# A hybrid backbone layer on eight cores: block 0 of the first feed-forward without its down products, and the latents' second norm woven into the context's projections

## The chip, the cores and the metric

One Trainium2 chip, all 8 NeuronCores, one program. Each core does its own share and none talks to another. The metric is the device time of one execution in microseconds (us), which is that of the slowest core. A core has TensorE (PE, matmuls), VectorE (DVE), ScalarE (ACT), GpSimd (POOL) and SyncE (SP). POOL and SP also issue the DMAs. Each engine runs its own list of instructions strictly in order.

## What is computed

One layer of a diffusion backbone on 8192 context tokens and 8192 latent tokens of width 1024:

```
x += 0.5 * gate1 * SwiGLU1(mod(rmsnorm(x)))                  # FF1, hidden width 2816
h  = mod(rmsnorm(x)); [p | q | k | v | gate logits] = h @ w_in
A  = PoolMixer(p) @ w_br_pool                                # centred mean over 2/4/8/16 tokens
B  = Attn(q, k, v) @ w_br_att                                # context: dense; latent: neighbourhood + cache
x += gate2 * ((sig_A * A + sig_B * B) @ w_out)
x += 0.5 * gate3 * SwiGLU2(mod(rmsnorm(x)))                  # FF2
```

`mod` is a scale and a shift per channel that come from a conditioning vector (`ada` weights). The outputs are x of both kinds of tokens and the context's k and v.

## The kernel before

**Tiles.** A core holds 1024 context tokens (half 0), 1024 latent tokens (half 1) and 256 neighbouring latent tokens. They stand as five token tiles: 0 and 1 are context, 2 and 3 latents, 4 the 256 neighbours (`TT_ALL`). x lies transposed, channels on partitions, in eight chunks of 128 channels per tile: `XT[0..3]` in f32, `XH` for tile 4. `XN` holds the normed input of the next products in bf16. All of it, with the scratch, is one SBUF tensor, `arena`; PSUM is `ps`, eight banks of 512 f32 columns. Sharing of memory is kept by `P.claim`, which hands the waits of the old users to the new ones.

**Order of the work.** Python code emits the instructions of all engines; `P.emit` adds the semaphore waits that reads and writes need. An engine's order is the order of emission. Where two strands shall overlap, they are generators: `weave` (line 210) draws from a side strand in proportion to the cost of the main one, and `pump` (line 729) draws so many steps.

**Weights.** `plan` writes one list of 512 KB weight units; a ring of eight slots is filled in that order by POOL's DMA queue. `wacq` takes the next unit, `wrel` frees its slot, and the load into the slot waits for the last matmul that read it. Units 0 to 7 are ada weights; 8 and 9 are the gate and up weights of FF1's block 0, 10 to 13 ada weights, 14 its down weights, 15 to 17 those of block 1.

**A norm** (`norm_gen`, line 620) of a tile squares the eight chunks into `XN` (ACT, DVE or POOL by the string `sq`), sums them on PE with eight matmuls against ones (`norm_stat`, in bank 4 or 5), takes Ln and Exp on ACT, multiplies each chunk with the result on DVE or POOL into one of two buffers (`scaled`), and applies scale and shift from there into `XN` on ACT or DVE (`modulated`). ACT must load a table when it goes from Silu to Ln and when it goes back.

**Feed-forward** (`ff_phase`, line 723). The hidden width is cut in 11 blocks of 256. For a block and a tile, `ff_GU` makes the gate and up products of one 128-wide part `jj` (16 matmuls of 512 columns in two banks of 0 to 3), ACT takes Silu, DVE multiplies into `HB` (two slots). `ff_DN` makes the down products: for each of eight output chunks `m` two matmuls into a bank of `poolDN` (4 to 7), which DVE adds into x (`vstt`, line 430). Within a block, step s emits GU(s, 0), DN(s-1) chunks 0 to 3, GU(s, 1), DN(s-1) chunks 4 to 7. In FF1's block 0 x is still being loaded by SP's queue (`load_x_tile`, each tile after a given weight unit has landed), and the norm of tile s+1 is emitted inside step s. In FF1's last block, a tile that is done (`tile_done`) is spilled to DRAM and its second norm joins the side strands.

**Mixer** (`mixer`, line 1226). It first runs out the norms of tiles up to 2 (`left[0][0] <= 2`), then weaves: the context's q projection with the norms of tiles 3 and 4; the context's k and v projections with its pool branch (`p_gen(0)`); the latents' q, k, v projections (pool `d2`, banks 4, 5, 6) with the context's attention (`ctx_att`, banks 0 to 3); then the merge of the context and the latents' attention, and so on. A q or k product (`qk_gen`, line 834) is a group of eight matmuls in a bank; ACT squares it; `finish` of the group before it is emitted right after: one matmul with `ONESBLK` (pool `s2`, bank 7), Ln and Exp on ACT, and a `vstt` on DVE that reads the group's bank last. q, k and v of the two halves lie in the memory of x tiles that have been spilled: half 0 in that of tiles 2 and 3, half 1 in that of tiles 0 and 1.

In the traces, line 413 is `mm`, line 410 `mm` of attention, 422 `actv`, 426 `vtt`, 430 `vstt`, 603 `ptt` (POOL), 323 a weight load, 555 a load of x.

## Time and profile before

| | us |
|---|---|
| median of 3 runs (lowest, highest) | 1688.76 (1687.05, 1701.29) |
| the profiled execution's own time | 1701.97 |
| span of its slowest core, core 3 | 1700.4 |
| span of its core 0 | 1685.8 |

The page of the profile is of core 3. In this execution cores 2 and 3 had a lower granted clock than the other six, whose spans are 1680.7 to 1686.5 us; stretches below are read on core 0. Times in the rows are us from the span's start. A row of a timeline names the engine, the line and shape, the count of instructions merged, and in brackets how long the engine had been idle and what ended that.

### The profile page before, as it was taken

What the parts mean: (1) busy time and instruction counts of PE and PEld (TensorE: products, weight loads), DVE (VectorE), ACT (ScalarE), POOL (GpSimd) and SP (SyncE); (2) the same over time, 40 slices, a digit from 0 to 9 for tenths busy, and PEclk for the clock granted to TensorE, in tenths of its full rate; (3) what the DMA queues carried; (4) which work ended last, traced back from release to release, by engine and by line L of the source; (5) the groups of instructions that cost most, each with busy time, mean ns of one, the idle gap of its engine ahead of it and who ended that gap; (6) DMA issues with size and microseconds to landing.
All of it is one profiled execution on the core that took longest, in us unless ns stands there. A gap on an engine that the chain in (4) does not pass through costs nothing.

```text
span 1700.4 us, 25281 instructions; the slowest of 8 cores (1680.7 to 1700.4 us)
## 1 busy us (share of the span) xinstructions
PE 1536.0 (90%) x8548; PEld 695.4 (41%) x8548; DVE 956.5 (56%) x1646; ACT 494.2 (29%) x739; POOL 158.2 (9%) x235
## 2 busy tenths in 40 slices
PE   1689999999999995698889888999999999999998
PEld 1234444444444442243434444444334444444443
DVE  2256556555566554464546665345366666666666
ACT  2651110111111125745636566235421111111110
POOL 2131000000000012300000000021210000000000
PEclk9799999999999997787889899999999999999999
DMA  9906442345432332457225355584322222222005
GB/s 183 243 1 91 75 67 37 48 74 76 75 48 43 59 87 99 101 116 142 37 56 120 99 113 113 138 186 75 50 38 38 37 38 38 38 38 38 13 1 198
DMA packets 35788, 134.68 MB, mean 79 GB/s; under 512 B 5072, under 2 KB 5200, under 8 KB 33616
## 3 DMA queue, kind: packets, MB, share of 16 engines
q0 software_dynamic: 22560, 79.88, 30.3%
q1 hardware_dynamic: 13104, 53.18, 9.3%
q8 instruction: 73, 1.20, 0.3%
q14 instruction: 51, 0.42, 0.1%
HBM read 191.95 MB, written 20.97 MB: 125 GB/s over the span
## 4 chain that ended last, share of the span: by engine, by line
PE 79%; DVE 6%; issue 5%; ACT 4%; DMA 4%; POOL 1%; DVEq 0%; ACTq 0%; SPq 0%; POOLq 0%
PE ps L413 76%; ACT arena L422 3%; DVE arena L430 3%; PE ps L410 3%; DMA arena<-wts 3%; DVE arena L426 2%; POOL arena L603 1%; DMA arena<-xin 1%; DVE arena L436 1%; ACT L422 1%; DVEq L183 0%; DVE arena L445 0%; DVE arena L442 0%; ACTq L183 0%; POOL arena L323 0%
## 5 line engine op out<-in xcount | busy, mean ns | idle before, releaser
L413 PE MATMUL ps<-arena 128*128 128x512 bf16 (+3 forms) x7108 | 1476.7, 363 | 132.9 <-DVE arena L430 53.5
L413 PEld LDWEIGHTS ps<-arena 128*128 128x128 bf16 x7108 | 646.7, 100 | 919.6 <-issue 336.8
L430 DVE SCALAR_TENSOR_TENSOR arena<-ps,arena 128x512 f32<-128x512 f32 (+2 forms) x860 | 562.5, 714 | 89.6 <-ACT arena L422 47.1
L422 ACT ACTIVATE arena<-ps 128x512 f32<-128x512 f32 (+4 forms) x418 | 266.1, 652 | 1045.8 <-PE ps L413 526.7
L426 DVE TENSOR_TENSOR arena<-arena,ps 128x512 bf16<-128x512 f32 (+1 forms) x198 | 130.2, 658 | 411.7 <-PE ps L413 382.4
L426 DVE TENSOR_TENSOR arena<-arena 128x512 f32<-128x512 f32 (+10 forms) x196 | 141.6, 738 | 114.9 <-ACT arena L422 89.3
L323 POOL DMA_DIRECT2D arena<-wts x150 | 79.9, 536 | 1255.5 <-PE ps L413 1025.0
L422 ACT ACTIVATE arena<-arena 128x512 bf16<-128x512 f32 (+6 forms) x230 | 165.6, 748 | 86.9 <-DVE arena L426 25.0
L410 PE MATMUL ps<-arena 128*128 128x65 bf16 (+3 forms) x1440 | 80.6, 214 | 25.5 <-DVE arena L436 16.0
L603 POOL TENSOR_TENSOR arena<-arena 128x512 bf16<-128x512 f32 (+3 forms) x77 | 75.9, 1010 | 186.4 <-ACT arena L422 99.3
L410 PEld LDWEIGHTS ps<-arena 64*128 64x128 bf16 (+1 forms) x1440 | 53.5, 98 | 79.0 <-issue 69.8
L430 DVE SCALAR_TENSOR_TENSOR arena<-arena,ps 128x512 f32<-128x512 f32 x64 | 43.8, 684 | 51.0 <-PE ps L413 45.3
L436 DVE TENSOR_SCALAR arena<-ps,arena 128x64 bf16<-128x64 f32 (+1 forms) x136 | 38.0, 280 | 18.7 <-PE ps L413 3.6
L422 ACT ACTIVATE arena<-ps,arena 128x512 f32<-128x512 f32 (+2 forms) x66 | 43.5, 664 | 13.5 <-PE ps L413 12.5
L422 ACT ACT_TABLE_LOAD x25 | 32.1, 1283 | 46.2 <-PE ps L413 43.2
L442 DVE CAST arena<-ps 128x128 bf16<-128x128 f32 (+2 forms) x58 | 22.3, 391 | 19.7 <-PE ps L410 11.3
L442 DVE COPY arena<-ps 128x512 f32<-128x512 f32 x16 | 11.0, 687 | 7.1 <-PE ps L413 3.7
L442 DVE CAST arena<-arena 128x512 bf16<-128x512 f32 x16 | 6.8, 425 | 9.1 <-ACT arena L422 8.1
L430 DVE SCALAR_TENSOR_TENSOR arena<-arena 128x1024 bf16<-128x1024 f32 (+1 forms) x14 | 10.8, 770 | 1.0 <-DVE arena L426 0.2
L426 DVE TENSOR_TENSOR arena<-ps,arena 128x6 f32<-128x6 f32 (+2 forms) x20 | 3.3, 165 | 14.1 <-PE ps L413 13.1
L445 DVE RECIPROCAL arena<-ps 128x2 f32<-128x2 f32 (+1 forms) x48 | 8.0, 167 | 0.8 <-PE ps L410 0.8
L438 DVE TENSOR_SCALAR arena<-arena 128x512 bf16<-128x512 f32 x4 | 1.9, 542 | 0.1
(12 smaller groups left out, 6.1 us busy)
## 6 DMA issues: line engine op xcount, KB each, us to landing
arena<-wts POOLq DMA_DIRECT2D x150, 512.0 KB, 8.8
arena<-xin SPq DMA_DIRECT2D x8, 1024.0 KB, 13.6
xspill<-arena SPq DMA_DIRECT2D x4, 2048.0 KB, 7.0
arena<-xspill SPq DMA_DIRECT2D x4, 2048.0 KB, 14.7
yoT<-arena SPq DMA_DIRECT2D x32, 256.0 KB, 2.3
arena<-ebias SPq DMA_DIRECT2D x12, 640.0 KB, 5.1
arena<-ebias SPq DMA_DIRECT2D x8, 768.0 KB, 5.4
nkT<-arena SPq DMA_DIRECT2D x8, 256.0 KB, 2.9
```

What stands on the lines that cost most here:

```text
L323: wtok.append(P.emit("pool", lambda e: e.dma_start(out=WR[:, s, :], in_=src), writes=[wslot_res[s]], dma_sem="w%d" % s))
L410: return P.emit("pe", lambda e: e.matmul(out, lhsT=lhsT, rhs=rhs, start=start, stop=stop, skip_group_check=True), reads=reads, writes=writ ...
L413: return P.emit("pe", lambda e: e.matmul(out, lhsT=lhsT, rhs=rhs, start=start, stop=stop), reads=reads, writes=writes, inc=inc)
L422: return P.emit("act", lambda e: e.activation(out=out, in_=in_, func=func, **kw), reads=reads, writes=writes)
L426: return P.emit("dve", lambda e: e.tensor_tensor(out=out, in0=in0, in1=in1, op=op), reads=reads, writes=writes)
L430: return P.emit("dve", lambda e: e.scalar_tensor_tensor(out=out, in0=in0, scalar=scalar, in1=in1, op0=op0, op1=op1), reads=reads, writes=w ...
L436: return P.emit("dve", lambda e: e.tensor_scalar(out=out, in0=in0, scalar1=s1, scalar2=None, op0=op0), reads=reads, writes=writes)
L438: return P.emit("dve", lambda e: e.tensor_scalar(out=out, in0=in0, scalar1=s1, scalar2=s2, op0=op0, op1=op1), reads=reads, writes=writes)
L442: return P.emit("dve", lambda e: e.tensor_copy(out=out, in_=in_), reads=reads, writes=writes)
L445: return P.emit("dve", lambda e: e.reciprocal(out=out, in_=in_), reads=reads, writes=writes)
L603: return P.emit("pool", lambda e: e.tensor_tensor(out=out, in0=in0, in1=in1, op=op), reads=reads, writes=writes)
```

## The change

It has two parts, made together.

*FF1 block 0.* All five tiles' gate and up products are made without down products between them; their hidden values go to `HB5` (slots 2 to 6), and the down products (`owed`) are emitted in block 1, chunk by chunk beside block 1's own. In block 0 the squares of a tile are emitted two tiles ahead, those of tile 1 ahead of tile 0's Ln; `modulated` alternates between ACT and DVE. The loads of x tiles wait for earlier units, that of tile 1 for a later one. The four ada units of the hook are used after all of block 0's products.

*Second norm.* In FF1's last block only tiles 0 and 1 (context) are normed. The norms of tiles 2, 3 and 4 are woven into the context's q, k and v projections. The memory is swapped to allow it: half 0's q, k, v lie over x tiles 0 and 1, half 1's over 2 and 3. The context's pool branch moves into the weave with the latents' projections and the context's attention; there the latents' projections keep banks 4 and 5, and the pool branch has bank 6. The context's projections have banks 0 to 3 where they had 0 to 5. A norm with a gap takes bank 4 alone, and down products use banks 5 to 7 while a norm may be beside them and in each last block.

```diff
-        for nm in ("q", "k", "p", "v"):
+        for nm in ("q", "k", "v"):
             plan_win(0, nm)
-        for nm in ("q", "k", "v"):
-            plan_win(1, nm)
+        plan_win(1, "q")
+        plan_win(0, "p")
+        plan_win(1, "k")
+        plan_win(1, "v")
...
+        HB5 = mem(oG + 16384, 10240, BF16, "p (t j n) -> p t j n", t=5, j=2)
...
-            b = stat if stat is not None else norm_stat(tile)
+            b = stat if stat is not None else norm_stat(tile, 4 if gap else None)
...
+        def hbuf(hs):
+            return (HB, "hb", hs) if hs < 2 else (HB5, "hb5", hs - 2)
...
         poolDN = PsumPool(P, [4, 5, 6, 7], "DN")
+        poolDN3 = PsumPool(P, [5, 6, 7], "DN3")
...
-                while k > 0 and side:
+                while k > 0 and side and not (lazy_load is not None and side[0][0] > 1):
...
-                for ti, u in ((1, 6), (2, 10), (3, 13), (4, 15)):
+                for ti, u in ((1, 7), (2, 9), (3, 10), (4, 11)):
                     lazy_load(ti, after=wtok[u])
+                norm_tile(nidx, tiles[1], part="a", sq="apv")
                 norm_tile(nidx, tiles[0], part="b", mo="av", stat=stat0, mid=lambda: first_mod(acc))
...
+                if first:
+                    for t in range(ntt):
+                        ff_GU(G, U, rg, ru, nj, tiles[t], 2 + t, jjs=[0])
+                        if t + 2 < ntt:
+                            norm_tile(nidx, tiles[t + 2], part="a", sq="pppapppa")
+                        if t + 1 < ntt:
+                            norm_tile(nidx, tiles[t + 1], part="b", mo="av")
+                        ff_GU(G, U, rg, ru, nj, tiles[t], 2 + t, jjs=[1])
+                    wrel(ug)
+                    wrel(uu)
+                    blk0_hook()
+                    owed = wacq(("ffd", which, bi))
+                    after_block(bi)
+                    continue
...
-                        if first and step + 1 < ntt:
-                            norm_tile(nidx, tiles[step + 1], sq="a" if step == 0 else "pppppppa",
-                                      sc="vvvp" if step else "v")
-                        if first and step == 1:
-                            blk0_hook()
-                            ud, Dn, rd = wacq(("ffd", which, bi))
...
+                        if owed is not None and step < ntt:
+                            ff_DN(owed[1], owed[2], nj, tiles[step], 2 + step, ig, ms=[m])
                         if step >= 1:
                             ff_DN(Dn, rd, nj, tiles[step - 1], (step - 1) % 2, ig, ms=[m],
-                                  chunk_done=chunk_done if last else None)
-                            pump(3 if last else 2)
+                                  chunk_done=chunk_done if last else None, spare=bool(side) or last)
+                            pump(2)
...
-            while left and left[0][0] <= 2:
+            while left and left[0][0] < 2:
                 run_all(left.pop(0)[1])
...
-            d1, s1 = PsumPool(P, [0, 1, 2, 3, 4, 5], "d1"), PsumPool(P, [6, 7], "s1")
-            weave(qk_gen(0, "q", d1, s1), 16.0, side, 40.0)
...
-            weave(chain_gens(qk_gen(0, "k", d1, s1), v_gen(0, d1)), 30.0, p_gen(0, d1), 21.0)
...
+            d1, s1 = PsumPool(P, [0, 1, 2, 3], "d1"), PsumPool(P, [6, 7], "s1")
+            weave(chain_gens(qk_gen(0, "q", d1, s1), qk_gen(0, "k", d1, s1), v_gen(0, d1)), 46.0, side, 78.0)
...
-            d2, s2 = PsumPool(P, [4, 5, 6], "d2"), PsumPool(P, [7], "s2")
-            weave(chain_gens(qk_gen(1, "q", d2, s2), qk_gen(1, "k", d2, s2), v_gen(1, d2)), 54.0, ctx_att(), 32.0)
+            d2, s2 = PsumPool(P, [4, 5], "d2"), PsumPool(P, [7], "s2")
+            weave(weave_gen(chain_gens(qk_gen(1, "q", d2, s2), qk_gen(1, "k", d2, s2), v_gen(1, d2)), 54.0,
+                            p_gen(0, PsumPool(P, [6], "d2p")), 21.0), 75.0, ctx_att(), 32.0)
...
-            return norm_gen(1, TT_ALL[ti], sc="vvvp", gap=4)
+            if ti < 2:
+                return norm_gen(1, TT_ALL[ti], sq="pppa", sc="vvvp", gap=4)
+            return norm_gen(1, TT_ALL[ti], sq="p", sc="vvvp", mo="av", gap=4)
```

ACT at the start, before: the small one is the conditioning vector's Silu, the four that follow are tile 0's squares, then Ln (`ps,arena`), Exp and four `modulated` of tile 0, Silu, and the eight squares of tile 1.

```order
L422 ACTIVATE arena<-arena 128x16
L422 ACTIVATE arena<-arena 128x512 x4
L422 ACTIVATE arena<-ps,arena 128x512
L422 ACTIVATE arena<-arena 128x512 x5
L422 ACTIVATE arena<-ps 128x512
L422 ACTIVATE arena<-arena 128x512 x8
```

The same place after the change (lines have moved by two):

```order
L424 ACTIVATE arena<-arena 128x16
L424 ACTIVATE arena<-arena 128x512 x7
L424 ACTIVATE arena<-ps,arena 128x512
L424 ACTIVATE arena<-arena 128x512 x5
L424 ACTIVATE arena<-ps 128x512
L424 ACTIVATE arena<-arena 128x512 x2
```

Three squares of tile 1 now stand ahead of tile 0's Ln, where none did.

PE at the first weave of the latents' projections with the context's attention, before: `128x256 x4` are score products, `128x65 x8` products with v, `128x128 x2` transposes, `128x512 x9` a group of eight for q with the `ONESBLK` matmul of the group before it.

```order
L410 MATMUL ps<-arena 128x256 x4
L413 MATMUL ps<-arena 128x512 x9
L410 MATMUL ps<-arena 128x256 x4
L413 MATMUL ps<-arena 128x512 x9
L410 MATMUL ps<-arena 128x65 x8
L413 MATMUL ps<-arena 128x512 x9
L410 MATMUL ps<-arena 128x256 x4
L413 MATMUL ps<-arena 128x512 x9
L410 MATMUL ps<-arena 128x65 x8
L410 MATMUL ps<-arena 128x128 x2
```

The same place after the change; `x8` is a group of the pool branch, `x17` and `x18` are two groups of q in a row.

```order
L412 MATMUL ps<-arena 128x256 x4
L415 MATMUL ps<-arena 128x512 x17
L412 MATMUL ps<-arena 128x256 x4
L415 MATMUL ps<-arena 128x512 x9
L412 MATMUL ps<-arena 128x65 x8
L415 MATMUL ps<-arena 128x512 x8
L412 MATMUL ps<-arena 128x256 x4
L415 MATMUL ps<-arena 128x512 x18
L412 MATMUL ps<-arena 128x65 x8
L412 MATMUL ps<-arena 128x128 x2
```

Some neighbouring q groups have a pool group between them, others only attention products, and some nothing.

## Rows read from the trace of the kernel before

**Rows 1.** The page: busy time and share, and PE and its clock in 40 slices.
```profile
PE 1536.0 (90%) x8548; PEld 695.4 (41%) x8548; DVE 956.5 (56%) x1646; ACT 494.2 (29%) x739; POOL 158.2 (9%) x235
...
PE   1689999999999995698889888999999999999998
...
PEclk9799999999999997787889899999999999999999
```

**Rows 2.** Busy time by stretch, core 0 (length, then each engine, clock, DMA).
```profile
604.00:694.00 90.00, 64.70 (x273) 27.87 (x277) 45.98 (x79) 44.91 (x65) 24.22 (x23) 0.85 0.29 101
694.00:776.00 82.00, 67.28 (x282) 28.87 (x286) 47.72 (x76) 49.48 (x85) 11.80 (x19) 0.92 0.50 107
776.00:832.00 56.00, 46.50 (x311) 21.35 (x314) 26.26 (x72) 41.47 (x68) 3.12 (x7) 0.94 0.53 97
```

**Rows 3.** Timeline of core 0, the first tiles of FF1's block 0.
```profile
32.67 4.90 DVE L426 TENSOR_TENSOR arena<-arena 128x512 f32<-128x512 f32 x8 [8.69 <-ACT arena L422]
...
35.66 19.62 SPq L555 DMA_DIRECT2D arena<-xin  x4
...
38.62 0.57 PE L413 MATMUL ps<-arena 128*128 128x2 bf16 x16 [2.33 <-DMA arena<-wts]
...
44.00 3.19 PE L413 MATMUL ps<-arena 128*128 128x512 bf16 x7 [4.82 <-ACT arena L422]
...
49.41 2.75 PE L413 MATMUL ps<-arena 128*128 128x512 bf16 x12 [2.22 <-DMA arena<-wts]
...
53.56 2.19 ACT L422 ACTIVATE arena<-arena 128x512 bf16<-128x512 f32 x4 [2.32 <-DMA arena<-xin]
```

**Rows 4.** The same timeline: tile 2's wait for x, down products' `vstt`, end of block 0.
```profile
72.84 0.63 ACT L422 ACTIVATE arena<-arena 128x512 bf16<-128x512 f32 x1 [3.45 <-DMA arena<-xin]
...
86.83 14.04 PE L413 MATMUL ps<-arena 128*128 128x512 bf16 x51 [4.82 <-DVE arena L426]
...
88.15 2.73 DVE L430 SCALAR_TENSOR_TENSOR arena<-ps,arena 128x512 f32<-128x512 f32 x4
...
133.62 0.59 POOL L323 DMA_DIRECT2D arena<-wts  x1 [8.26 <-PE ps L413]
...
141.47 0.60 ACT L422 ACTIVATE arena<-ps 128x512 f32<-128x512 f32 x1 [7.80 <-PE ps L413]
```

**Rows 5.** The same timeline, tile 1's norm: table load, Ln, Exp, first and last chunks.
```profile
56.55 1.28 ACT L422 ACT_TABLE_LOAD   x1 [0.81 <-PE ps L413]
...
57.85 0.69 ACT L422 ACTIVATE arena<-ps,arena 128x512 f32<-128x512 f32 x1
...
58.63 0.63 ACT L422 ACTIVATE arena<-arena 128x512 f32<-128x512 f32 x1
59.36 1.29 DVE L426 TENSOR_TENSOR arena<-arena 128x512 f32<-128x512 f32 x2 [7.26 <-ACT arena L422]
...
65.47 1.52 ACT L422 ACTIVATE arena<-arena 128x512 bf16<-128x512 f32 x2 [0.25 <-DVE arena L426]
```

**Rows 6.** Timeline of core 0, FF1's last block around GU(3, 0).
```profile
644.54 0.60 ACT L422 ACTIVATE arena<-ps 128x512 f32<-128x512 f32 x1
...
645.31 0.69 DVE L426 TENSOR_TENSOR arena<-arena,ps 128x512 bf16<-128x512 f32 x1 [3.63 <-ACT arena L422]
...
646.81 7.89 PE L413 MATMUL ps<-arena 128*128 128x512 bf16 x23 [3.97 <-DVE arena L430]
```

**Rows 7.** Timeline of core 0: a dense stretch of PE, then latents' projections beside the context's attention.
```profile
720.78 21.11 PE L413 MATMUL ps<-arena 128*128 128x512 bf16 x95 [0.69 <-ACT arena L422]
...
783.75 0.60 ACT L422 ACTIVATE arena<-ps 128x512 bf16<-128x512 f32 x1 [0.30 <-PE ps L413]
...
785.89 0.74 DVE L430 SCALAR_TENSOR_TENSOR arena<-ps,arena 128x512 bf16<-128x512 f32 x1
...
791.33 0.52 PE L410 MATMUL ps<-arena 128*128 128x65 bf16 x10 [2.12 <-DVE arena L442]
...
791.68 3.77 PE L413 MATMUL ps<-arena 128*128 128x512 bf16 x9
```

80 lines of the change are left out of this document (44 added, 36 removed).

## The prediction

> **What bounds the kernel now.** I read the page first. PE is busy 90% of the span, and in its 40 slices it dips in two places: the first three slices, and slices 15 to 17 (600 to 720 us), where the granted clock dips too [rows 1]. So outside these PE sets the pace, and work moved there costs its own length. The table by stretches says how much is to be had: from 604 to 694 us, FF1's last block with the second norms, PE is busy 64.7 of 90 us, and 67.3 of 82 in the context's projections after it; in the next stretch, the latents' projections with the context's attention, 46.5 of 56 [rows 2]. The count of matmuls gives the rest. A dense matmul of 512 columns takes 0.222 us (95 in 21.11) [rows 7]. From 603.6 to 776.5 PE has 532 of them or their like (216 of the block, 36 sums for norms, 280 for q, k, v, p), 118 us of 172.9. So 55 us are waiting or half clock.
>
> The timelines name the waits. In FF1's last block, GU(3, 0)'s Silu stands on ACT behind all eight `modulated` of a norm and a table load; DVE waits 3.63 us for that Silu and behind it hold all evictions, so PE waits 3.97 us for a bank, and its next 23 matmuls take 7.89 us, 0.34 each [rows 6]. At the start, tile 0's first product begins at 44.0 and the up weights come at 49.4 (2.22 us of waiting), x of tile 1 is whole at 53.6, x of tile 2 at 72.8 [rows 3, 4]. Block 0 ends at 140.0: the first Silu of block 1 is at 141.5, after eight gate products (1.7 us) [rows 4].
>
> **The start.** Tile 1's load now waits for unit 7 instead of 6. Unit 7 landed at 38.6, where the last ada matmuls run; the first of the four loads of tiles 1 and 2 was issued at 35.66, when unit 6 was there [rows 3]. That is 2.9 us; unit 7 lands a little sooner without x beside it, so I take x of tile 1 whole 2 us later, at 55.6. That would harm nothing, but ACT now has three squares of tile 1 ahead of tile 0's Ln, and DVE two of them ahead of tile 0's `scaled`, and the last ones need the second half of x. Before, Ln and the eight `scaled` were done under the ada loads (32.7 to 37.6) [rows 3]. Now they come in a row: square 0.6, table, Ln and Exp 2.8 [rows 5], eight `scaled` 4.9, biases and four `modulated` on ACT 4.1 (they lie in PE's wait of 4.82 before 44.00) [rows 3], to 68.0. Eight up matmuls at 0.43 (the rate after 44.00, too [rows 3]) end at 71.4; it was about 51.
>
> Then the norm of the next tile bounds each step: eight sums, table with Ln and Exp 2.8, eight chunks 7.6 (59.4 to 67.0) [rows 5], eight up matmuls. Half the chunks on DVE don't shorten this: DVE then has two `scaled` and a `modulated` per pair, about what ACT had. Sums and up products take 1.8 us each dense and 3.4 at half clock; I take 2.5 and 3. The first step ends at 87.5 (x of tile 2, 73 us, comes in time), two more of 15.7 at 119, the 256 columns of tile 4 need 10, the last products and the ada matmuls 5: block 0 ends at 134, 6 us earlier than now. At full clock it is 126, at half throughout 139.
>
> What is owed: 4.5 tiles by 16 matmuls are 72 by 0.222 = 15.8 us, in block 1, where PE is dense. DVE must take two evictions where it took one, 16 by 0.68 [rows 4] and two products of 0.69 = 12.3 us per tile against PE's 64 by 0.222 = 14.2: covered for the big tiles, short by some 1.3 us for tile 4. Block 1's up weights wait for the slot of block 0's gate weights. Before, that load was issued at 133.6 and was there when needed 7.8 us later [rows 4], under down products; now only up products, ada matmuls and a gate group cover it, some 5 us: 2 us lost (0 to 4). Sum for the start: -6 + 15.8 + 1.3 + 2 = **+13.1 us** (+5 to +19).
>
> **The second norm.** In the last block norms 0 and 1 stay, at fewer steps per chunk, so Silu(3, 0) stands behind three `modulated` and not eight. By hand from these durations: PE waits 4.7 us and loses 1.7 to the clock in step 3, some 8.5 in step 4 and at the evictions of the end. 232 matmuls are 51 us, with that 66: the block ends at 669.6 instead of about 693. Then q, k, v of the context with norms 2, 3, 4. ACT has Square, Ln, Exp per group, 1.9 us, and a norm's Ln, Exp and four `modulated` of 0.76 [rows 5], 4.4 us in 7.4 groups (its 25 steps at 78/46 steps per unit of cost, a group being 2): 2.5 us per group, where PE has 2.2. So 16 groups take 40 us at ACT's pace, the eight of v 16 at PE's: 56, to 726. The next stretch starts 50 us earlier. But the pool branch, 72 matmuls or 15.8 us, is not yet done: **-34.2 us** (-40 to -26). Four banks instead of six don't bind here.
>
> **The latents' projections with two banks.** This is the price. A q or k group's bank is read last by `vstt`, which is emitted after the next group. From the next group's end to the end of that `vstt` the trace has Square at 783.75 to `vstt`'s end at 786.63, 2.9 us [rows 7]. With three banks another group of 1.75 us and attention products lay between; with banks 4 and 5 the group after next waits for it. What is woven between is 0.2 (`ONESBLK`) and 0.4 to 0.7 of attention, and a pool group of 1.75 us in about five places of 14 (the second order of PE shows both kinds). So a period is 2.9 + 1.75 = 4.65 us, where 20 groups had 56 us, 2.8 each, and some 2 us of PE stand idle in most. No row of before shows such a row of waits. From below: at the full clock, 14 by 4.65, the first two groups 3.9, four groups of 256 columns by 3.2: 82 us against the 56 now [rows 2], less seven pool groups absorbed (12.2), +13.6. From above: after a gap of 2.12 us the next nine matmuls took 3.77 us, half clock [rows 7]; if each unfilled wait does that, 9 periods of 6.4, 5 of 5.9, with the rest 108 us, and 0.6 us per period for `vstt` behind the pool branch's long DVE adds: +48. I take five half-clock groups (8.5 us), 0.3 us of DVE queue per period (4), and 2 us for pool mixes that share one bank: 82 + 8.5 + 4 + 2 - 56 - 12.2 = **+28 us**.
>
> The Trainium skill, "TensorE: Matmul & The Clock Gate", on the failure mode called psum-queue depth-cycling, says that cycling through PSUM banks with small idles between groups makes the clock oscillate and costs throughput. The row of 2.12 us agrees; by that rule the second rival below would be the case. "Perfetto Trace Analysis", on matmuls, says that groups should rotate through banks so that eviction overlaps the next group. Two banks do rotate; by that rule there would be no loss (the first rival), but the rows make eviction longer than the next group.
>
> **Sum.** Core 0's span 1685.8 and 1.6 around it (1701.97 - 1700.4) are 1687.4, 1.4 under the median 1688.76. 13.1 - 34.2 + 28 = +6.9, so 1695.7. FF2's last block with three banks is bound by the same DVE evictions as with four: 0 to 2 us, taken as 0.
>
> **Rivals.**
> *The two banks cost nothing to speak of.* Pool and attention work fills the waits, as the DVE and ACT are only half busy there. For it: PE is idle 9.5 us of the 56 now anyway [rows 2]. Against: five fills for 14 periods. The third term is then +2: 13.1 - 34.2 + 2 = -19.1, 1669.7. An earlier x of tile 1 would go the same way.
> *Half clock after each two-bank wait.* The place is the latents' q and k. It decides from the point where an unfilled wait keeps the clock down as the 2.12 us did: a wait of 0.69 us ahead of the dense stretch did not [rows 7], and I expect some 2.2. The third term is +48: +26.9, 1715.7.
> *ACT holds the context's projections.* If q, k, v with three norms takes 70 us and not 56, for `modulated` ahead of Square and PE waiting for POOL's squares, the second term is -20: +21.1, 1709.9. For it: ACT and PE are within 15% there.
> That the change does not do what it says: the orders show it does, but the squares ahead of tile 0's Ln undo block 0's gain; that is in the forecast.
>
> **How the numbers follow.** Forecast 0.50 (its own range 1680 to 1706), no bank cost 0.17, half clock 0.23, ACT 0.10. What a measurement of this kernel can tell from no change is about 1%, 17 us: 1672 to 1706. The forecast lies within it, the first rival under, the two others over: faster 0.17, same 0.50, slower 0.33. The range runs from just under the first rival to just over the second: 1668 to 1718.
>
> **What would show it.** Right: tile 0's Ln after 55 us and its gate products near 65; block 1's first Silu between 128 and 140, and block 1 some 15 us longer than block 2; the first score products of attention near 740 (726 and the start's 13); then PE idle 2 us before most q and k groups with `vstt` (L432) as releaser, and more L415 matmuls of 0.43 us. Wrong: Ln of tile 0 at 32; a stretch of latents' projections under 75 us; or score products of attention after 755.

## The result, and the profile after

| | before | after |
|---|---|---|
| runs compared, us | 1687.05, 1688.76, 1701.29 | 1749.22, 1750.65 |
| median of all four, us | 1695.03 | 1780.08 |
| ratio of the runs compared, 95% interval | | 1.034 (1.0227 to 1.0453) |
| span of core 0, us | 1685.8 | 1733.3 |
| span of the slowest core, us | 1700.4 | 1747.7 |

The change makes the kernel slower by 3.4%. The prediction was 1695.7, range 1668 to 1718: wrong, and outside the range. (The medians of all four hold runs, 1823.58 before and 1809.51 and 1942.15 after, in which the cores of one die had a lower clock; the ratio leaves them out, and the table by run leaves out the rest of e4's profiled execution for the same reason.)

The page after, of core 6, answers to [rows 1]: PE is busy 87% where it was 90%, its second slice stands at 2 instead of 6, and seven slices from 655 us on stand at 6 or 7, where two stood at 5 and 6.

```profile
PE 1525.1 (87%) x8391; PEld 695.1 (40%) x8548; DVE 983.0 (56%) x1682; ACT 465.5 (27%) x693; POOL 173.4 (10%) x245
...
PE   1278999999999997777677889899999999999998
...
PEclk9978999999999998888889999899999999999999
```

The same table by stretch as [rows 2], core 0 after, cut at these marks: first Silu of FF1's block 1, of block 2, of the last block; the context's first Square; the first score product of the context's attention; the first of the latents' attention; the end.

```profile
0.00:142.30 142.30, 62.38 (x394) 29.01 (x400) 51.34 (x90) 47.45 (x66) 36.42 (x48) 0.76 0.60 131
142.30:217.20 74.90, 70.02 (x364) 30.55 (x371) 55.08 (x92) 5.55 (x11) 4.71 (x9) 0.98 0.35 60
217.20:631.10 413.90, 397.79 (x2219) 194.21 (x2256) 248.16 (x422) 44.37 (x81) 23.77 (x45) 0.98 0.37 62
631.10:700.10 69.00, 56.08 (x252) 24.58 (x256) 39.84 (x63) 27.50 (x38) 19.55 (x20) 0.90 0.38 127
700.10:771.10 71.00, 56.24 (x227) 23.38 (x230) 35.21 (x57) 43.07 (x71) 29.12 (x33) 0.88 0.43 106
771.10:910.40 139.30, 94.14 (x547) 42.44 (x558) 71.70 (x166) 56.32 (x88) 7.09 (x13) 0.89 0.30 60
910.40:1733.30 822.90, 775.10 (x4396) 347.37 (x4480) 480.07 (x794) 240.99 (x341) 52.73 (x79) 0.98 0.33 74
```

These marks cut every run below in the same way; this is the table to keep at hand (core 0, us; "after" predicted is what the prediction's terms make of before: its stages come 0.8 over its sum of +6.9, as it cut the stages a little elsewhere). "2 to 9" are the eight blocks between block 1 and the last. What each run changes is told in the sections below.

| run | block 0 | block 1 | 2 to 9 | last | context | latents | rest | ratio to before (95%) |
|---|---|---|---|---|---|---|---|---|
| before | 141.5 | 50.7 | 413.2 | 93.3 | 77.9 | 86.3 | 823.0 | |
| after, predicted | 135.5 | 69.8 | 413.2 | 66 | 56 | 130.1 | 823.0 | 1.004 |
| after | 142.3 | 74.9 | 413.9 | 69.0 | 71.0 | 139.3 | 822.9 | 1.034 |
| e1 block 0's part alone | 145.5 | 76.8 | 414.3 | 93.1 | 79.6 | 86.7 | 821.9 | 1.0197 (1.0181 to 1.0212) |
| e5 | 139.2 | 77.9 | 414.4 | 93.3 | 77.9 | 86.2 | 821.8 | 1.0146 (1.0098 to 1.0195) |
| e16 | 128.9 | 75.1 | 417.4 | 93.0 | 79.5 | 86.7 | 821.2 | 1.0064 (1.0029 to 1.0099) |
| e6 | 147.7 | 81.3 | 414.3 | 93.3 | 77.9 | 86.6 | 819.6 | 1.0195 (1.0127 to 1.0263) |
| e15 | 145.0 | 68.6 | 412.3 | 93.1 | 79.6 | 86.7 | 820.8 | 1.0113 (1.0076 to 1.015) |
| e2 second norm's part alone | 139.6 | 51.4 | 412.3 | 68.5 | 72.8 | 141.2 | 824.4 | 1.0166 (1.0128 to 1.0204) |
| e8 | 139.6 | 50.7 | 410.0 | 68.5 | 72.8 | 132.3 | 824.6 | 1.0105 (1.0069 to 1.0141) |
| e10 | 138.8 | 51.8 | 415.1 | 69.0 | 74.3 | 137.2 | 824.4 | 1.0119 (1.0051 to 1.0186) |
| e12 | 139.9 | 52.5 | 412.6 | 68.5 | 72.8 | 120.8 | 823.2 | 1.0043 (1.0031 to 1.0056) |
| e11 | 139.8 | 52.5 | 412.7 | 68.5 | 118.5 | 69.7 | 825.0 | 1.0011 (0.9979 to 1.0042) |
| e13 | 140.2 | 50.7 | 409.9 | 68.5 | 115.4 | 64.5 | 822.4 | 0.9943 (0.9927 to 0.9959) |
| e20 | 140.6 | 51.8 | 412.1 | 68.5 | 114.7 | 65.0 | 823.9 | 0.9877 (0.9857 to 0.9897) |
| e17 before, early read | 139.8 | 51.5 | 412.2 | 93.3 | 80.7 | 81.3 | 825.4 | 0.992 (0.9902 to 0.9938) |
| e14 | 143.0 | 52.5 | 415.3 | 69.7 | 114.0 | 64.9 | 823.5 | 0.9943 (0.9925 to 0.9961) |
| e22 | 140.6 | 52.5 | 412.5 | 68.5 | 124.6 | 65.1 | 823.8 | 1.0016 (1.0007 to 1.0025) |
| e21 | 133.9 | 72.7 | 415.2 | 69.9 | 114.3 | 65.0 | 822.5 | 1.003 (1.0018 to 1.0042) |
| e3 | 146.3 | 75.2 | 412.6 | 69.9 | 108.3 | 83.6 | 824.0 | 1.0236 (1.0219 to 1.0253) |
| e4 two banks alone | 140.4 | 50.7 | 410.0 | 93.3 | 77.9 | 131.9 | | 1.0276 (1.0256 to 1.0297) |

Each ratio is taken against runs of the kernel before made beside it. Their median was 1687.96 beside e1 to e4, 1690.72 beside e5, e6, e8 and e10, 1691.14 beside e11 to e14, 1702.45 beside e15, e16, e17 and e20, and 1689.95 beside e21 and e22; the ratios of e15, e16, e17 and e20 therefore flatter by some 0.7%.

The table also shows how far a stage moves where nothing was changed in it: the context's stage of before's order is 77.9 or 79.6 us, block 0 of before's order lies between 138.8 and 143.0, and blocks 2 to 9 between 409.9 and 417.4. Smaller differences than these say nothing.

The prediction was made from core 0. Its 47.5 us are 25.7 up to the last block, -24.3 in that block, -6.9 in the context's stage and +53.0 in the latents' stage. In that execution core 0 is the fastest core of all: block 0 ends at 142.3 there and at 144.6 to 146.8 on the others, whose spans reach 1747.7. This is why the timed difference (61 us against the median of the three, 1688.76) is larger than core 0's.

### The profile page after: what moved, and what is told of

The parts are those of the page before. It is cut to its first block, busy times and chain, and to the rows that moved or that the text cites. A ratio compares the mean times of both kernels' runs of the same rounds, so it can differ in the third digit from the quotient of the medians.

```text
span 1747.7 us, 25134 instructions; the slowest of 8 cores (1733.3 to 1747.7 us)
## 1 busy us (share of the span) xinstructions
PE 1525.1 (87%) x8391; PEld 695.1 (40%) x8548; DVE 983.0 (56%) x1682; ACT 465.5 (27%) x693; POOL 173.4 (10%) x245
## 4 chain that ended last, share of the span: by engine, by line
PE 75%; DVE 8%; issue 7%; ACT 5%; DMA 3%; POOL 2%; DVEq 0%; another core or an unknown queue 0%; ACTq 0%; SPq 0%; POOLq 0%
PE ps L415 72%; ACT arena L424 4%; DVE arena L432 4%; PE ps L412 3%; DVE arena L428 3%; DMA arena<-wts 2%; POOL arena L607 1%; DMA arena<-xin 1%; DVE arena L438 1%; ACT L424 1%; DVE arena L440 0%; POOL arena L323 0%; DVEq L183 0%; DVE arena L444 0%
## 5 line engine op out<-in xcount | busy, mean ns | idle before, releaser
L415 PE MATMUL ps<-arena 128*128 128x512 bf16 (+2 forms) x6951 | 1461.4, 362 | 197.2 <-ACT arena L424 76.7
L428 DVE TENSOR_TENSOR arena<-arena 128x512 f32<-128x512 f32 (+10 forms) x204 | 150.4, 757 | 122.2 <-ACT arena L424 65.5
L424 ACT ACTIVATE arena<-arena 128x512 bf16<-128x512 f32 (+6 forms) x184 | 137.9, 765 | 117.5 <-DMA arena<-xin 48.0
L607 POOL TENSOR_TENSOR arena<-arena 128x512 bf16<-128x512 f32 (+3 forms) x87 | 90.9, 1070 | 160.3 <-ACT arena L424 66.0
L412 PE MATMUL ps<-arena 128*128 128x65 bf16 (+3 forms) x1440 | 80.4, 214 | 20.7 <-DVE arena L438 15.8
L424 ACT ACTIVATE arena<-ps,arena 128x512 f32<-128x512 f32 (+2 forms) x66 | 43.4, 663 | 14.8 <-PE ps L412 5.4
L424 ACT ACT_TABLE_LOAD x25 | 32.1, 1283 | 45.9 <-PE ps L415 42.8
L440 DVE TENSOR_SCALAR arena<-arena 128x512 bf16<-128x512 f32 (+1 forms) x32 | 19.9, 629 | 6.0 <-POOL arena L607 3.4
L428 DVE TENSOR_TENSOR arena<-ps,arena 128x6 f32<-128x6 f32 (+2 forms) x20 | 3.3, 165 | 13.6 <-PE ps L415 12.6
L447 DVE RECIPROCAL arena<-ps 128x2 f32<-128x2 f32 (+1 forms) x48 | 8.0, 166 | 1.1 <-PE ps L412 1.0
## 6 DMA issues: line engine op xcount, KB each, us to landing
arena<-xspill SPq DMA_DIRECT2D x4, 2048.0 KB, 11.8
```

Source lines behind the costliest of these rows:

```text
L412: return P.emit("pe", lambda e: e.matmul(out, lhsT=lhsT, rhs=rhs, start=start, stop=stop, skip_group_check=True), reads=reads, writes=writ ...
L415: return P.emit("pe", lambda e: e.matmul(out, lhsT=lhsT, rhs=rhs, start=start, stop=stop), reads=reads, writes=writes, inc=inc)
L424: return P.emit("act", lambda e: e.activation(out=out, in_=in_, func=func, **kw), reads=reads, writes=writes)
L428: return P.emit("dve", lambda e: e.tensor_tensor(out=out, in0=in0, in1=in1, op=op), reads=reads, writes=writes)
L440: return P.emit("dve", lambda e: e.tensor_scalar(out=out, in0=in0, scalar1=s1, scalar2=s2, op0=op0, op1=op1), reads=reads, writes=writes)
L447: return P.emit("dve", lambda e: e.reciprocal(out=out, in_=in_), reads=reads, writes=writes)
```

## The experiments

### Each half alone, and the two banks alone

e1 is block 0's part with the rest as before, e2 the rest with block 0 as before. e3 gives the latents' projections three banks again and weaves the pool branch with the context's v. e4 is the kernel before with one list changed:

```diff
-            d2, s2 = PsumPool(P, [4, 5, 6], "d2"), PsumPool(P, [7], "s2")
+            d2, s2 = PsumPool(P, [4, 5], "d2"), PsumPool(P, [7], "s2")
```

> Block 0 in two parts with its down products in block 1, alone; last block, context's projections and latents' projections as before. Core 0 of the kernel before ends at 1685.8 us; in the changed kernel the first Silu of the last block comes 25.7 us later (631.1 against 605.4). Theory (the three terms stand apart, and this one is 25.7 us): core 0 ends near 1711, some 1.5% over the kernel before. Rival (a part of the 25.7 us is lost only because the last block follows it differently, or is made up later by weights that are there sooner): under 1700, or over 1720.

> Second norm between the context's projections, pool branch and two banks in the latents' projections, with block 0 as before. Theory (terms stand apart): the last block ends some 24 us sooner, context's q, k, v take 71 us without the pool branch, the latents' stage 139 us: -24.3 - 6.8 + 53.0 = +22, core 0 ends near 1708, and together with the block 0 run the two differences make the 47.5 us of both at once. Rival (they interact, for instance by the clock or by when weights come): the sum of both differences is off by over 8 us.

> The changed kernel, but the latents' projections have banks 4, 5, 6 again and the pool branch is woven with the context's v instead of the latents' projections (norms 2, 3, 4 lie between the context's q and k only). Theory (two banks made the 37 us net of the latents' stage): that stage goes from 139 us back to some 86, the context's stage grows by the pool branch's 15.8 us and little else (71 to 87-92): core 0 ends at 1733.3 - 53.0 + 16 to 21 = 1696 to 1701. Rival (the stage is long for the pool branch's adds on DVE or for the clock, not for banks): the stage with three banks stays over 105 us or the adds cost as much beside v; end over 1712.

> The kernel before with banks 4 and 5 instead of 4, 5, 6 for the latents' projections, nothing else changed (bank 6 idle). The stage from the first score product of the context's attention to the first of the latents' is 86.3 us in the kernel before, 56 of it projections. Theory (each bank is read last by vstt 2.9 us after the next group's end, period 4.65 us): without the pool branch's groups between them at least 14 periods lose about 1.8 us: +26 us if at the full clock, up to +50 if the half clock follows; I expect +35, core 0 ends near 1721. Rival (the two banks are covered by attention and it is the pool branch, its one bank and its DVE adds that make the stage long): +10 or less, end under 1697.

Measured: in the timed runs the halves add up. They lie 33 and 25 us over those of the kernel before, together 58 of the 61. On core 0 alone they don't: 32.1 and 24.5 against the 47.5 of both, 9 us off. e1's own term on core 0 is 31 us, not 25.7, like the other cores of the change; core 0 did better than these in the one profiled execution after.

e4 is the clearest of the four: one bank fewer, and the stage goes from 86.3 to 131.9 us, +45.6 where +35 was expected, with nothing else in it. The timed runs say the same (1734.7 and 1735.3 against 1688). For the same matmuls PE's busy time goes from 71.8 to 89.0 us and its idle time from 14.5 to 42.9, so 17 of the 45.6 us are the clock. e3's latents' stage is back at 83.6, as that theory has it, but its context's stage is 108.3 instead of the 87 to 92 expected; core 0 ends at 1719.9, 13 us sooner than with the change (the timed runs lie 22 us lower), where 32 to 37 were expected. The pool branch costs more than its 15.8 us of products beside v, too: at its end PE waits 6.55 us for its adds on DVE. So a part of e3's rival held: the adds cost as much beside v.

### What the latents' stage waits for

PE after, core 0, the first periods of the latents' q (the timeline's columns as in [rows 7]):

```profile
782.93 2.10 PE L415 MATMUL ps<-arena 128*128 128x512 bf16 x9 [0.48 <-DVE arena L447]
787.81 2.10 PE L415 MATMUL ps<-arena 128*128 128x512 bf16 x9 [2.78 <-DVE arena L432]
...
792.69 2.99 PE L415 MATMUL ps<-arena 128*128 128x512 bf16 x9 [2.41 <-DVE arena L447]
...
803.61 3.65 PE L415 MATMUL ps<-arena 128*128 128x512 bf16 x9 [2.45 <-DVE arena L432]
```

From group to group 4.88 us (782.93 to 787.81, 787.81 to 792.69), with a wait of 2.4 to 2.8 us for the `vstt` that reads the bank two groups back, and then nine products in 3.0 to 3.65 us in some and 2.1 in others. (L447, named in two rows, is the attention's reciprocal right behind that `vstt` on DVE. The `vstt` ends at 792.54 and PE starts 0.15 us later, as it does at 787.81 behind the one that ends at 787.66.) Is it the number of banks, or how late that read is issued? e8 makes 4, 5 and 6 one pool for both kinds of groups. e12 leaves the banks as they are and issues the read earlier:

```diff
                             mm(bank_ap(b)[:, 0:n], W[:, kc, bb * 128:(bb + 1) * 128], XN[:, kc, t0:t0 + n],
                                kc == 0, kc == 7, [rw, rxn(kc, t0)], [banks[b]], inc=(kc == 7))
+                            if kc == 3 and half == 1 and pend:
+                                finish(pend.pop(0))
```

> The run with the second norm's part alone, with one edit: banks 4, 5 and 6 are one pool that the latents' projections and the pool branch share, instead of 4, 5 for the one and 6 for the other; the order of all engines is the same. That run's stage from the context's first score product to the latents' first takes 141.2 us (86.3 before, without the pool branch's 15.8); with two banks alone and no pool branch it took 131.9. Theory (the third use of a bank, 2.9 us behind the next group, is what makes it wait; a third bank removes most waits): stage 104 to 112 us, timed 1677 to 1684, faster than the kernel before. Rival (the pool branch's adds on DVE and the mix through ACT hold the evictions, whatever the banks): 125 us or more, timed over 1696.

> The run with the second norm's part alone (two banks for the latents' projections, one for the pool branch), with one edit: in the latents' q and k the sum over a head's squares, Ln, Exp and vstt of a group are issued behind the fourth product of the next group instead of behind its eighth. Nothing else moves. The stage took 141.2 us there. With three banks shared it still took 132.3, so the number of banks is not the whole of it. Theory (what counts is how late the read that frees the bank is issued and done, 2.9 us behind the next group's end): four products are 0.9 us, in some 14 periods, and fewer stretches at the lower clock: stage 122 to 131 us. Rival (the evictions are late for other work on ACT or DVE, not for the order on PE): stage within 3 us of 141.

e8 fell short: 132.3 us, where 104 to 112 were expected. With a pool group between two q groups, three shared banks are two again; this is read from the order, not tested by itself. (By the order of emission, two of the latents' k groups in e8 and e10 read their successor's sums: where two pool mixes lie between them, they have the same bank. The times are read with that in mind; the order of work is the same.)

e12 is the answer: 120.8 us instead of 141.2, for four matmuls of order. (On ACT the move does a little more: Ln and Exp of a group now stand ahead of the next group's Square.) From group to group it is 3.80 us (760.20 to 764.00 below) where it was 4.88 after the change. The table by stretches for this stage, core 0, first e2:

```profile
744.70:885.90 141.20, 98.23 (x548) 43.61 (x558) 71.00 (x164) 55.57 (x87) 7.10 (x13) 0.85 0.31 59
```

and e12 (this window begins 0.7 us ahead of its mark; at the mark the busy time is 86.3 and the clock the same):

```profile
745.50:866.30 120.80, 86.42 (x548) 40.13 (x557) 72.05 (x167) 55.97 (x88) 7.10 (x13) 0.96 0.37 72
```

The same 548 matmuls are in both. PE's idle time falls from 43.0 to 34.4 us, 8.6, less than 14 times 0.9; the matmuls themselves fall from 98.2 to 86.4 us, 11.8, as the granted clock of the stretch rises from 0.85 to 0.96. The greater part of this gain was the clock, which the shorter waits gave back. e12's rows show waits of 1.3 to 1.6 us with full speed behind them:

```profile
752.11 2.10 PE L415 MATMUL ps<-arena 128*128 128x512 bf16 x9 [1.39 <-DVE arena L432]
...
760.20 2.10 PE L415 MATMUL ps<-arena 128*128 128x512 bf16 x9 [1.64 <-DVE arena L432]
...
764.00 2.10 PE L415 MATMUL ps<-arena 128*128 128x512 bf16 x9 [1.34 <-DVE arena L447]
```

The Trainium skill, "TensorE: Matmul & The Clock Gate", has this under psum-queue depth-cycling: small idles between groups that cycle through banks make the clock oscillate. The trace agrees in part: the clock was 0.85 with waits mostly of 2.3 to 2.8 us and 0.96 with mostly shorter ones, but not every such wait was followed by half clock (787.81 above).

The stage has a second part, which neither run touches. Its q and k products end at 832.6 before and at 868.5 after; behind that only v, the attention and, after, the rest of the pool branch are left. Before:

```profile
776.50:832.60 56.10, 46.27 (x310) 21.42 (x316) 26.19 (x71) 41.98 (x69) 3.02 (x6) 0.94 0.53 97
832.60:862.80 30.20, 25.51 (x167) 11.44 (x171) 19.08 (x56) 6.09 (x8) 1.06 (x2) 0.90 0.31 53
```

and after, with PE's two long waits of the second part:

```profile
771.10:868.50 97.40, 64.70 (x368) 29.43 (x374) 46.72 (x108) 47.61 (x77) 4.45 (x8) 0.89 0.28 59
868.50:910.40 41.90, 29.44 (x179) 13.01 (x184) 24.97 (x60) 8.71 (x12) 2.64 (x5) 0.88 0.34 64
```

```profile
883.73 2.10 PE L415 MATMUL ps<-arena 128*128 128x512 bf16 x9 [1.93 <-ACT arena L424]
...
895.57 4.00 PE L415 MATMUL ps<-arena 128*128 128x512 bf16 x9 [5.14 <-ACT arena L424]
```

So of the stage's 53.0 us, 41.3 lie in the q and k part and 11.7 in the other. The two waits are for the pool branch's last mixes: ACT reads their one bank after DVE has done the branch's adds (888.53 to 893.80), the same chain as the 6.55 us in e3. In the whole stage PE's idle time grew by 30.6 us and its busy time by 22.4, of which 15.5 are the pool branch's 72 products at full clock: on this core the clock cost some 7 us more than before.

### The context's stage

e10 (on e8) takes the `modulated` of norms 2 to 4 off ACT, e14 (on e13, below) gives half their squares to DVE, e20 (on e13) gives the context's projections five banks and the early read.

```diff
-            return norm_gen(1, TT_ALL[ti], sq="p", sc="vvvp", mo="av", gap=4)
+            return norm_gen(1, TT_ALL[ti], sq="p", sc="vvvp", mo="v", gap=4)
```

> The run with shared banks, with one more edit: the modulated chunks of norms 2, 3 and 4 (between the context's projections) all on DVE instead of half on ACT. The context's stage took 72.8 us without the pool branch in the run with the second norm's part alone, PE waiting for ACT before 2.6, 2.1, 2.7 and 2.1 us at its single products (the sum of squares per head, which needs Square). Theory (Square stands behind modulated on ACT): the stage shortens by 4 to 8 us against the shared banks' run. Rival (PE waits for the norm's own chain, POOL's squares and Ln, or the work only changes the engine): within 2 us, or longer, since DVE's scaled and modulated then stand ahead of vstt.

> Those two edits, and the squares of norms 2, 3 and 4 half on DVE and half on POOL instead of all on POOL (1.0 us each). In the context's stage (72.8 us) PE waits 0.6 to 0.8 us ahead of single products of the norm's sum, for POOL's squares. Theory (POOL's squares pace the sums): stage shorter by 3 to 6 us. Rival (ACT is what paces the stage, with Square, Ln, Exp and modulated in one queue): within 2 us.

> The run with the pool branch beside the latents' q and the early read there, with two more edits: the early read in the context's q and k too, and five banks (0, 1, 2, 3, 5) instead of four for the context's projections. The stage with q, k, v and three norms took 72.8 us of the 115.4 us from the context's first Square to the latents' first score product. Theory (the late read with four banks paces the context's stage, not ACT's modulated or POOL's squares): 5 to 10 us less, timed 1673 to 1678. Rival (the chain of each norm, from squares to modulated, paces it): within 2 us of that run.

None of the three moved it by much: 74.3 instead of 72.8 in e10; 114.0 and 114.7 instead of 115.4 with q and pool branch in e14 and e20. (Read to the latents' first Square, which leaves most of q and the pool branch out, e14's stage is 72.0 where runs with the same order there have 74.3 to 76.1, so some 3 us shorter; but PE's waits in it add up to 14.8 us against 14.7 in e13, and what shrank is its busy time.) What PE waits for merely changes its name. In e2 (the timeline of ACT and PE, first fence) it waits for ACT's Square, which stands behind a `modulated` that itself waited for DVE; in e10 (PE, second fence) for DVE's `vstt`, which stands behind `modulated` and `scaled` there.

```profile
688.63 0.81 ACT L424 ACTIVATE arena<-arena 128x512 bf16<-128x512 f32 x1 [1.50 <-DVE arena L428]
...
690.07 0.38 PE L415 MATMUL ps<-arena 128*128 128x512 bf16 x1 [2.63 <-ACT arena L424]
```

and e10:

```profile
695.37 2.10 PE L415 MATMUL ps<-arena 128*128 128x512 bf16 x9 [1.57 <-DVE arena L432]
...
729.43 1.89 PE L415 MATMUL ps<-arena 128*128 128x512 bf16 x8 [3.63 <-DVE arena L432]
```

After, PE waits 11.6 us for ACT and 2.8 for POOL in this stage and is busy 56.2 of 71.0 us at a clock of 0.88, while ACT is busy only 43.1. That the chain of a norm through POOL, PE, ACT and DVE, in queues shared with Square and `vstt`, sets the 71 us is what remains; it was not tested by itself and stays open.

### Block 0: squares ahead of a norm

After, ACT and DVE at tile 0's norm, core 0:

```profile
49.29 1.15 ACT L424 ACTIVATE arena<-arena 128x512 bf16<-128x512 f32 x2 [25.59 <-DMA arena<-xin]
55.08 0.63 ACT L424 ACTIVATE arena<-arena 128x512 bf16<-128x512 f32 x1 [4.65 <-DMA arena<-xin]
55.73 1.28 ACT L424 ACT_TABLE_LOAD   x1
57.02 0.69 ACT L424 ACTIVATE arena<-ps,arena 128x512 f32<-128x512 f32 x1
```

then DVE's `scaled`:

```profile
58.53 6.59 DVE L428 TENSOR_TENSOR arena<-arena 128x512 f32<-128x512 f32 x8 [2.75 <-ACT arena L424]
```

ACT waits 25.59 us for x of tile 1 with tile 0's Ln behind it in the queue. e5 moves tile 1's squares behind tile 0's norm, and e16 in addition the squares of tile t + 2 behind the norm of tile t + 1:

```diff
                         if t + 1 < ntt:
                             norm_tile(nidx, tiles[t + 1], part="b", mo="av")
+                        if t + 2 < ntt:
+                            norm_tile(nidx, tiles[t + 2], part="a", sq="pppapppa")
```

> The run with block 0 in two parts alone, with one edit: tile 1's squares are issued behind tile 0's norm instead of ahead of its Ln and scaled. In that run PE stands idle 29.57 us before tile 0's first product at 68.33 (40.00 to 44 in the kernel before), and the first Silu of block 1 is at 145.5. Theory (the squares ahead of Ln hold tile 0's norm until x of tile 1 is whole at some 55 us, and what follows is shifted by it): first product back near 44, tile 1's chunks at 59 to 67 instead of 77 to 92, and block 0 then bound by x of tile 2 at 73 and three norms of 15.7 us: block 0 ends 8 to 14 us sooner, 132 to 138, timed 1708 to 1714. Rival (x tiles and weights bound block 0 anyway): 3 us or less, 1718 or more.

> The run with tile 1's squares behind tile 0's norm, with one more edit: inside block 0 the squares of the tile after next are issued behind the next tile's norm instead of ahead of it. In that run tile 1's Ln stood at 70.80 on ACT behind two squares of tile 2 that waited for x until 62.55 and 68.86, while tile 1's own squares were done at 57, and the four later tiles follow in steps of 16 to 20 us; block 0 took 139.2 and 136.8 us. Theory (ACT's queue, not x or weights): tile 1's Ln at 59 to 61, block 0 ends at 126 to 132. Rival (x of tile 2, whole at 69, then bounds the rest): 135 or more.

e5 gave 6.3 us on core 0 (9.2 on core 4, 146.0 to 136.8; 7.7 in the median of the eight cores), less than the 8 to 14 expected, since the same fault was there once more: tile 1's Ln, with its squares done, stood behind two squares of tile 2 (ACT in e5).

```profile
68.86 0.63 ACT L422 ACTIVATE arena<-arena 128x512 bf16<-128x512 f32 x1 [5.68 <-DMA arena<-xin]
69.51 1.28 ACT L422 ACT_TABLE_LOAD   x1
70.80 0.69 ACT L422 ACTIVATE arena<-ps,arena 128x512 f32<-128x512 f32 x1
```

With e16 that Ln is at 60.05 and block 0 ends at 128.9, 10 us sooner than in e5. Core 0 flatters here: the eight cores end at 128.2 to 134.6, in the median 133.0 against 137.9, 5 us sooner. Two places in in-order queues, not x or weights, had held block 0 for some 13 us together. The weights come in right behind: in e16 PE waits 1.0 to 3.4 us for block 1's up weights, by core, and 1.13 on core 0 of the change.

### Block 1: eight evictions in a row

The Silus of block 1 tell its pace. After, core 0, half a tile takes 7.62 us (161.55 to 169.17), and the releaser named is DVE's `vstt`:

```profile
161.55 0.60 ACT L424 ACTIVATE arena<-ps 128x512 f32<-128x512 f32 x1 [7.03 <-DVE arena L432]
169.17 0.60 ACT L424 ACTIVATE arena<-ps 128x512 f32<-128x512 f32 x1 [7.03 <-DVE arena L432]
```

Dense it would be 32 products, 6.91 us at the 0.216 of before's block 1 (24 products in 5.18). e6 issues DVE's product of Silu and up behind an eviction or two; e15 puts the down products in runs of four, between gate and up products as well.

```diff
+                            ff_GU(G, U, rg, ru, nj, tiles[step], step % 2, jjs=[jj],
+                                  mid=lambda jj: downs((4 * jj, 4 * jj + 1)))
+                            downs((4 * jj + 2, 4 * jj + 3))
```

> The run with block 0 in two parts alone, with one edit: in block 1 the product of Silu and up (DVE) is issued behind the next one or two evictions instead of ahead of them. Block 1 took 76.8 us there against 50.7 before, where the owed products are 72 by 0.222 = 16 us. Theory (DVE's product, waiting for Silu ahead of the evictions, delays banks and costs PE some 5 us): block 1 in 71 to 73 us, timed 1716 to 1717. Rival (DVE's own rate on tile 4's evictions, 0.21 to 0.28 us of waiting per four products from 207 us on, and the wait of 2.14 us for the up weights make the surplus): block 1 stays within 2 us of 76.8.

> The run with block 0 in two parts alone, with one edit: in block 1 the down products go in runs of four (two of each kind) behind the gate products and behind the up products, instead of in runs of eight behind both. Half a tile took 7.62 us there, 32 products dense are 6.91. Theory (eight down products in a row, made every 0.43 us and read by DVE every 0.67, overrun their four banks): half a tile in 6.91, block 1 shorter by 4 to 6 us than 76.8. Rival (DVE's or ACT's total work, or tile 4's end): 75 us or more.

e6 refuted my first reading: 8.05 us per half tile, worse. e15 confirmed the second (ACT again):

```profile
162.72 0.60 ACT L422 ACTIVATE arena<-ps 128x512 f32<-128x512 f32 x1 [6.31 <-PE ps L413]
169.62 0.60 ACT L422 ACTIVATE arena<-ps 128x512 f32<-128x512 f32 x1 [6.31 <-PE ps L413]
```

6.90 us, and the releaser named is PE. Block 1 is 68.6 us, 8.2 less than in e1, where 4 to 6 were expected. DVE had time enough on the average (55 of 75 us busy), but eight pairs come in 3.5 us and leave in 5.4 (0.67 each; eight took 5.35 in e1). Four banks hold the difference for a run of four and not for one of eight.

### What is worth keeping

e11 weaves the pool branch with the latents' q on six banks before the context's attention starts, so that only k and v, on three banks, stand beside the attention; e13 adds the early read, e17 makes only the early read, in the kernel before. e22 weaves the pool branch faster (36 for 21), e21 puts e15's and e16's start ahead of e20.

```diff
+            d6 = PsumPool(P, [0, 1, 2, 3, 4, 5], "d6")
+            weave(qk_gen(1, "q", d6, s1), 16.0, p_gen(0, d6), 21.0)
+            d2, s2 = PsumPool(P, [4, 5, 6], "d2"), PsumPool(P, [7], "s2")
+            weave(chain_gens(qk_gen(1, "k", d2, s2), v_gen(1, d2)), 38.0, ctx_att(), 32.0)
```

> The run with the second norm's part alone, with one edit: the latents' q is woven with the pool branch on six banks before the context's attention begins, and only the latents' k and v are woven with the attention, on banks 4, 5, 6. Theory (few banks beside the attention make the loss): from the context's first Square to the latents' first score product it took 72.8 + 141.2 = 214 us; now 72.8, then 128 products of q and pool in 30 to 36 us, then k, v and attention, 86.3 less q's share of some 14, in 70 to 78 us: 175 to 186 together, core 0 ends near 1677, timed 1675 to 1683, a little faster than the kernel before. Rival (the pool branch's adds hold evictions wherever it stands, as beside v of the context, where v and pool took some 40 us for 30 of products): 190 us or more, no faster than the kernel before.

> Both edits of the last two runs together. If the late read is what holds k's groups beside the attention even with three banks, another 2 to 6 us less than with the pool branch moved alone; if three banks hide it there, within 1 us of that run.

> The kernel before with one edit: in q and k of both halves, the sum over a head's squares, Ln, Exp and vstt of a group are issued behind the fourth product of the next group instead of the eighth. The latents' stage (86.3 us, three banks) should lose what it lost when the pool branch stood elsewhere, about 5 us (69.7 to 64.5); the context's stage (77.9, six banks) little, 0 to 3. Timed 1680 to 1685. Rival (with three and six banks the late read is hidden): within 2 us of 1688.

> The run with five banks, with one edit: the pool branch is woven faster than the latents' q (weight 36 instead of 21 against q's 16), so that its adds on DVE lie under q's last products. The stage from the context's first Square to the latents' first score product took 114.7 us, of which some 42 are q and pool branch, with waits of 1.8, 1.5 and 5.1 us for vstt behind the adds. Theory (the adds of the last groups pace the end): 3 to 6 us less, 109 to 112, timed about 4 us below that run. Rival (the adds take DVE time wherever they stand, and q's vstt wait behind them the same): within 1.5 us.

> The run with five banks with block 0 in two parts ahead of it, mended: tile 1's squares behind tile 0's norm, the squares of the tile after next behind the next tile's norm, and block 1's down products in runs of four. Stages measured alone: block 0 128.9 and 131.9 us, block 1 68.6, together 198 to 200 against 192 to 193 in the kernel before. Theory (stages add up): 5 to 8 us over the run with five banks, near the kernel before. Rival (the two mended parts hold on to one another, as block 1's up weights come later relative to an earlier block 0): 10 us or more over it.

e11 is level with before: 118.5 + 69.7 is 188 where 175 to 186 were hoped for, as q's `vstt` waits behind the pool branch's adds. e13 takes 8 us more off, where 2 to 6 were expected, and is faster than before, 0.9943. e17's context stage became 2.8 us longer and its latents' stage 5.0 shorter, so core 0 gained 1.6: the late read matters where banks are short. By absolute times (its ratio flatters, above) e17, at 1688, is level with before; e20, 1679 to 1685, is about where e13 and e14 are, 1680 to 1684, and only of these two is it shown that they are faster, by 0.6% (intervals 0.9927 to 0.9959 and 0.9925 to 0.9961). e22 was a miss, 124.6 instead of 114.7: PE now waits 1.88, 2.49, 3.87 and 5.41 us for q's `vstt`, so the adds hold q in both orders tried. e21 is slower than e20 by some 14 us on core 0 in its first two blocks (133.9 + 72.7; 9 on core 4, 12 between the medians of the cores), as its rival had it, and over the kernel before (1695.15 against 1689.95): even mended, block 0 in two parts costs more than it saves. Where the two mended parts hold on to one another was not found; PE waits 2.28 us for the up weights on core 0 and 0.29 on core 4.

## Why the prediction was wrong

**Right.** The last block: 69.0 us against 66. x of tile 1: whole at 55.1 (55.6 said), tile 0's first product at 67.83 (68.0), Ln of tile 0 after 55. Period of the two banks: 4.88 measured, 4.65 plus 0.3 said, waits of 2.4 to 2.8, and half clock behind some but not all of them. The signs and the places of all three terms held; the sizes did not.

**The step that failed most: "ACT at its pace, 56 us" for the context's q, k, v with three norms** (-34.2 for the second term; -24.3 - 6.9 + 15.8 = -15.4 measured). It took 71.0. I added up busy time per engine and took the larger; a chain through four engines in shared queues is longer than its busiest engine. By parts: the 16 groups of q and k took 51.9 us (to 751.97) and not 40, v 19.1 and not 16. The rival "ACT holds the context's projections" gave 70 us and was given a chance of 0.10. By its time it was right. Its two causes are in the rows, but neither is what sets the time alone: without `modulated` on ACT (e10) and with half the squares off POOL (e14) PE waited as long for something else.

**"Block 0 ends at 134, 6 us earlier"** (135.5 by the first Silu of block 1; measured 142.3). The norms' Ln stand at 75.47, 94.53, 111.03 and 126.95: steps of 16.5 and 15.9 where 15.7 was said, but 19.1 for the first, where its 71.4 to 87.5 make 16.1. There tile 1's chunks took 10.2 us instead of 7.6, and tile 0's eight `scaled` 6.59 instead of 4.90, while POOL squares beside them. Some 2.5 us more came behind the last Ln: 15.3 us to block 1's first Silu, where the prediction's steps leave about 13. The prediction did note that squares stand ahead of Ln; it took the loss as unavoidable within the change, and did not see the second such place, which e16 mended.

**"Covered for the big tiles: DVE 12.3 us per tile against PE's 14.2".** An average. Banks are held by the run, and a run of eight pairs is 5.4 us of DVE against 3.5 of PE. Block 1 was to grow by 19 us (15.8, 1.3 and 2) and grew by 24.2. e15 shows 6 to 8 of them gone. The 2 us for the up weights were 1.13.

**"+28 us for two banks"**: +37.2 (53.0 less 15.8). The mechanism held, and e4 shows it with nothing else in the way. For the q and k products themselves the size held too: 97.4 us where the prediction's 82 + 8.5 + 4 + 2 make 96.5. That is in part luck, since PE's idle time grew by 22.9 us there where 19.8 were said, and the clock cost some 6 where 8.5 were said. The miss lies behind them. The prediction had 2 us for the mixes that share a bank, within the 96.5, and put the adds that go before the last mixes at nothing. The second part of the stage took 41.9 us instead of 30.2, where 3.6 more were said, with waits of 1.93 and 5.14 us behind those adds. Sum of the misses on core 0: 12.6 + 18.8 + 9.2 = 40.6, which is 47.5 - 6.9.

Two readings of the prediction were a little off without harm: the dips of PE and its clock in [rows 1] are the 16th and 17th slices, 638 to 723 us and not 600 to 720, and a dense matmul is 0.216 us (24 in 5.18) and not 0.222.

**The range** was cut at the second rival. Three terms with errors of one sign were not thought of together, nor that the slowest of eight cores sets the time.

## What to carry to other kernels

Count banks against the longest run of products between two reads and against how late the last read of a bank is issued, not against averages; moving one small dependent product, with the read behind it, four matmuls forward gave 20 us here, more than half of it in clock. A side branch costs more than its products where the last of them wait for its adds on DVE: 7 us here, and moving it elsewhere (e3, e22) did not remove that. In an in-order queue, an instruction that waits for a load must not stand ahead of one that is ready: look at every engine to which the helper deals its parts. And where four engines pass work around, take the measured time of the nearest such chain instead of the busiest engine's sum.

## What the runs showed of the hardware

DVE and POOL slow one another when both multiply f32 tiles in SBUF. The eight `scaled` of tile 0 took 4.90 us before, when POOL issued only weight loads [rows 3], and 6.59 after. Single instructions of the trace show where: the first six take 0.69 us each, begun 0.60 apart, and the last two, with POOL squaring beside them from 61.58 on, 1.53 and 1.52 us. e2 has the same beside a POOL multiplication of the norm (DVE alone, POOL, DVE beside it):

```profile
684.75 0.69 DVE L428 TENSOR_TENSOR arena<-arena 128x512 f32<-128x512 f32 x1 [0.55 <-ACT arena L424]
...
689.14 1.26 POOL L607 TENSOR_TENSOR arena<-arena 128x512 f32<-128x512 f32 x1 [10.04 <-DVE arena L440]
...
689.55 1.41 DVE L428 TENSOR_TENSOR arena<-arena 128x512 f32<-128x512 f32 x1 [0.61 <-ACT arena L424]
```

POOL's squares of 128x512, after, took 1.48 us each beside DVE (first row) and 1.01 where DVE had nothing to do (second):

```profile
61.58 4.45 POOL L607 TENSOR_TENSOR arena<-arena 128x512 bf16<-128x512 f32 x3 [3.90 <-DMA arena<-xin]
...
73.71 3.03 POOL L607 TENSOR_TENSOR arena<-arena 128x512 bf16<-128x512 f32 x3 [2.95 <-DMA arena<-xin]
```

And a wait does not cost the clock by being there: of waits between 1.3 and 2.8 us ahead of nine products, those in e12 (1.39, 1.64, 1.34) left 2.10 us for the nine, and those after the change (2.41, 2.45) were followed by 2.99 and 3.65 in two places, but 2.78 by 2.10 in another.
